# Output powers in four parts behind the weight splits, late softmax scaling in the second attention, and conditioning pieces one block later

## Time and profile before

| | |
|---|---|
| median of 3 runs | 1544.14 us (1543.37 to 1545.25) |
| profiled execution, its own time | 1544.38 us |
| its span, first to last instruction | 1542.5 us |
| mean granted TensorE clock | 0.977 of full |
| PE busy (matmul) | 1457.6 us, 94% |
| DVE, ACT, POOL busy | 749.0, 614.5, 406.1 us |

### The profile page before, as it was taken

How to read it: one execution, slowest core, us unless ns; L and a number is a source line. 1 busy time by engine, 2 the same in 40 slices (tenths; PEclk the granted TensorE clock), 3 DMA queues, 4 the chain that set the end, 5 groups by cost and what they waited for, 6 DMA issues and landing times.

```text
span 1542.5 us, 25177 instructions
## 1 busy us (share of the span) xinstructions
PE 1457.6 (94%) x10880; PEld 1253.0 (81%) x10880; DVE 749.0 (49%) x921; ACT 614.5 (40%) x753; POOL 406.1 (26%) x324
## 2 busy tenths in 40 slices
PE   5799999988999997999799999999999989899999
PEld 5688889988999995765276888888886855799999
DVE  7975645365545466567654121212124577443343
ACT  4433364434333456121345222322224447544443
POOL 4977712100002410000000232343230020134553
PEclk9899999999999998999899999999999989999999
DMA  7466676544655564886434323222233310345552
GB/s 256 164 219 211 221 240 219 203 160 137 191 179 178 189 219 159 265 239 189 151 109 166 108 84 106 87 105 98 93 109 110 101 64 1 110 137 191 172 184 82
DMA packets 158259, 239.37 MB, mean 155 GB/s; under 512 B 5680, under 2 KB 128592, under 8 KB 158032
## 3 DMA queue, kind: packets, MB, share of 16 engines
q1 hardware_dynamic: 153360, 232.85, 45.4%
q10 hardware_dynamic: 4800, 5.08, 1.4%
HBM read 227.55 MB, written 1.05 MB: 148 GB/s over the span
## 4 chain that ended last, share of the span: by engine, by line
PE 84%; DVE 7%; ACT 6%; issue 2%; DMA 1%; POOL 0%; DVEq 0%; SPq 0%; ACTq 0%; POOLq 0%
PE bank L1968 24%; PE bank L1969 24%; PE bank L1970 24%; PE bank L2036 2%; PE bank L2273 2%; ACT A L589 1%; DVE wlo L1085 1%; ACT whi L633 1%; ACT ahi L593 1%; PE bank L2433 1%; PE bank L2110 1%; DVE stat L1713 1%; PE bank L563 1%; PE bank L544 1%; PE bank L2145 1%
## 5 line engine op out<-in xcount | busy, mean ns | idle before, releaser
L1968 PE MATMUL bank<-ahi,whi 128*128 128x256 f32 (+1 forms) x2480 | 792.7, 320 | 38.5 <-DVE wlo L1085 10.3
L1969 PE MATMUL bank<-alo,whi 128*128 128x256 f32 (+1 forms) x2480 | 784.1, 316 | 0.0
L1970 PE MATMUL bank<-ahi,wlo 128*128 128x256 f32 (+1 forms) x2480 | 783.4, 316 | 0.0
L1085 DVE TENSOR_TENSOR wlo<-raw,whi 128x2048 fp32r<-128x2048 f32 x158 | 362.2, 2292 | 533.1 <-ACT whi L633 533.0
L633 ACT ACTIVATE whi<-raw 128x2048 fp32r<-128x2048 f32 x160 | 306.3, 1914 | 726.2 <-PE bank L1970 726.2
L1968 PEld LDWEIGHTS bank<-ahi,whi 128*128 128x128 f32 x2480 | 477.8, 193 | 85.9 <-issue 40.9
L1970 PEld LDWEIGHTS bank<-ahi,wlo 128*128 128x128 f32 x2480 | 477.9, 193 | 28.8
L1969 PEld LDWEIGHTS bank<-alo,whi 128*128 128x128 f32 x2480 | 478.2, 193 | 27.8 <-issue 0.2
L1906 POOL TENSOR_TENSOR alo<-A,ahi 128x512 fp32r<-128x512 f32 (+1 forms) x43 | 125.8, 2927 | 351.8 <-ACT ahi L833 351.8
L1924 POOL TENSOR_TENSOR A<-A 128x512 f32 (+1 forms) x48 | 96.6, 2025 | 442.7 <-ACT A L956 442.7
L1560 DVE SCALAR_TENSOR_TENSOR A<-A,decay 128x512 f32<-128x512 f32 x80 | 53.8, 749 | 0.0
(11 more groups left out here) (302 smaller groups left out, 1200.8 us busy)
## 6 DMA issues: line engine op xcount, KB each, us to landing
raw<-in_w_ff SPq DMA_DIRECT2D x64, 1024.0 KB, 5.2
A<-in_w_mod SPq DMA_DIRECT2D x60, 512.0 KB, 4.7
raw<-in_w_in SPq DMA_DIRECT2D x28, 1024.0 KB, 8.2
modraw<-in_w_mod SPq DMA_DIRECT2D x36, 512.0 KB, 4.8
raw<-in_pw SPq DMA_DIRECT2D x12, 1024.0 KB, 8.4
raw<-in_w_ffn_gate SPq DMA_DIRECT2D x11, 1024.0 KB, 5.3
raw<-in_w_ffn_up SPq DMA_DIRECT2D x11, 1024.0 KB, 5.3
raw<-in_w_ffn_down SPq DMA_DIRECT2D x11, 1024.0 KB, 4.9
```

Source lines behind the costliest of these rows:

```text
L1085: dve.tensor_tensor(wlo[:, k % 2, :], raw[:, (k + 2) % 4, :], whi[:, k % 2, :].bitcast(F32), ALU.subtract).then_inc(wlo_ready, 1)
L1968: pe.matmul(out_, w_hi, a_hi, start=start, stop=False, **kw)
L1969: pe.matmul(out_, w_hi, a_lo, start=False, stop=False, **kw)
L1970: return pe.matmul(out_, w_lo, a_hi, start=False, stop=stop, **kw)
```

## The change

1. **Output powers.** DVE no longer makes those of batch 0 ahead of its block loop. Steps (3, 4) and (5, 6, 7) of batches 0 and 1 stand in the loop at l = 2, 3, 4, 5, each behind that l's `ahead`, so behind the splits of blocks 4 to 7.
2. **Convolution stage.** On PE, block 0 keeps pieces 4 to 7 only, and block l >= 1 has pieces 6 + 2l and 7 + 2l. Pieces 22, 23, 24 and 25 stand between `convolve(5)` and `convolve(6)`, 26 and 27 between the last two channel sums, 28 and 29 behind the sums of squares. Channel sums 4 and 5 come before `convolve(6)`, sum 6 before pieces 26 and 27. On ACT `ahead` stands before `mod_rows`. SP's program is unchanged.
3. **Second attention.** The probabilities are transposed and weighed unscaled. PE spreads the reciprocals over 64 rows with two small matmuls a step, ACT copies them to SBUF (`gspread`), DVE multiplies the 128x256 output of a pair of steps (`gnorm`), then ACT rounds (`gout`) and DVE subtracts (`glo`), one iteration later than before. From step 4 on, DVE copies one of the two transposed banks.
4. **Splits.** wlo of blocks 0 and 1 of "wo" is made by DVE (iteration 17, and behind the loop), not by POOL; ACT makes whi of block 1 in iteration 10.

```
             def act_pw1(p):
                 h = p.least // 2
+                ahead(p)
                 if p.least in (0, 4):
                     mod_rows(1, p.least // 4)
-                ahead(p)
...
                         act.wait_ge(pt_done, TR + i - 1)
+                        act.wait_ge(pn_ready, TR + i - 1)
...
                 if i >= 2:
                     act.wait_ge(o_done, TR + i - 1)
-                for s in range(2):
-                    c = act.activation(ptg[:, i % 2, 512 * s:512 * s + 512], pb[4 + s][:, :], ACT.Copy)
-                c.then_inc(pt_ready, 1)
+                if i < 4:
+                    act.activation(ptg[:, i % 2, 512:1024], pb[5][:, :], ACT.Copy).then_inc(pt_ready, 1)
+                act.activation(ptg[:, i % 2, 0:512], pb[4][:, :], ACT.Copy).then_inc(pt_ready, 1)
+
+            def gspread(c):
+                act.wait_ge(o_done, TR + 2 * c + 2)
+                if c >= 1:
+                    act.wait_ge(olo_ready, TR + 2 * c - 1)
+                act.activation(spd, pb[6 + c % 2][:, 256:512], ACT.Copy).then_inc(ohi_ready, 1)
 
             def gout(c):
-                act.wait_ge(o_done, TR + 2 * c + 2)
-                act.activation(ahi[:, 256 * c:256 * c + 256], pb[6 + c % 2][:, 0:256], ACT.Copy).then_inc(ohi_ready, 1)
-
-            for i in range(1, GSTEPS + 4):
+                act.wait_ge(olo_ready, TR + 2 * c + 1)
+                act.activation(ahi[:, 256 * c:256 * c + 256], onorm, ACT.Copy).then_inc(ohi_ready, 1)
+
+            for i in range(1, GSTEPS + 5):
                 if i - 1 < GSTEPS:
                     gexp(i - 1)
                 if i >= 5 and i % 2:
-                    gout((i - 5) // 2)
+                    gspread((i - 5) // 2)
+                if i >= 6 and i % 2 == 0:
+                    gout((i - 6) // 2)
                 if 0 <= i - 2 < GSTEPS:
                     gpt(i - 2)
-            ahead(Pos(FIRST["qkv"] + 5, 5))
+                if i == 10:
+                    ahead(Pos(FIRST["qkv"] + 5, 5))
...
-            dve.wait_ge(z_ready, 1)
-            dve.wait_ge(ssm_landed, 32)
-            output_powers(0, 3, 8)
...
                 ahead(Pos(l, l))
-                if l in (3, 4):
-                    output_powers(1, *((3, 5), (5, 8))[l - 3])
+                if l == 2:
+                    dve.wait_ge(z_ready, 1)
+                    dve.wait_ge(ssm_landed, 32)
+                if 2 <= l < 6:
+                    output_powers((l - 2) // 2, *((3, 5), (5, 8))[l % 2])
...
-            def gscale(i):
+            def ginvert(i):
                 s0, s1 = 20 + 2 * (i % 2), 36 + 2 * (i % 2)
                 dve.wait_ge(exp_done, TR + 2 * (i + 1))
-                link(dve.reciprocal(stat[:, s1:s1 + 2], stat[:, s0:s0 + 2]))
-                for b in range(2):
-                    m = dve.tensor_scalar(pg[:, i % 2, b, :], pg[:, i % 2, b, :], stat[:, s1 + b:s1 + b + 1],
-                                          None, ALU.mult)
-                m.then_inc(pn_ready, 1)
+                if i >= 2:
+                    dve.wait_ge(o_done, TR + i - 1)
+                dve.reciprocal(stat[:, s1:s1 + 2], stat[:, s0:s0 + 2]).then_inc(pn_ready, 1)
+
+            def gptb(i):
+                dve.wait_ge(pt_done, TR + i + 1)
+                dve.wait_ge(o_done, TR + i - 1)
+                dve.tensor_copy(ptg[:, i % 2, 512:1024], pb[5][:, :]).then_inc(pt_ready, 1)
+
+            def gnorm(c):
+                dve.wait_ge(ohi_ready, TR + 2 * c + 1)
+                if c >= 1:
+                    dve.wait_ge(olo_ready, TR + 2 * c)
+                dve.tensor_tensor(onorm, pb[6 + c % 2][:, 0:256], spd, ALU.mult).then_inc(olo_ready, 1)
...
                 if 0 <= i - 2 < GSTEPS:
-                    gscale(i - 2)
+                    ginvert(i - 2)
+                    if i - 2 >= 4:
+                        gptb(i - 2)
+                if i >= 6 and i % 2 == 0:
+                    glo((i - 6) // 2)
                 if i >= 5 and i % 2:
-                    glo((i - 5) // 2)
+                    gnorm((i - 5) // 2)
+                if i == GSTEPS + 1:
+                    ahead(Pos(FIRST["qkv"] + 4, 4))
+            ahead(Pos(FIRST["qkv"] + 5, 5))
...
-            split_ahead(4)
-            split_ahead(5)
...
                 if l == 0:
                     mod_pieces(4, 4)
-                mod_pieces(8 + 2 * l, 2)
+                else:
+                    mod_pieces(6 + 2 * l, 2)
             convolve(4)
             pe.wait_ge(u_ready, KD)
             for c in range(2):
                 channel_sum(c)
             convolve(5)
-            for c in range(2, 4):
+            for c in range(2, 5):
                 channel_sum(c)
+            mod_pieces(22, 2)
+            channel_sum(5)
+            mod_pieces(24, 2)
             convolve(6)
             mod_turn(1, 2)
-            mod_pieces(24, 2)
             convolve(7)
-            channel_sum(4)
-            channel_sum(5)
+            channel_sum(6)
             mod_pieces(26, 2)
-            channel_sum(6)
             channel_sum(7).then_inc(msum_done, 1)
-            mod_pieces(28, 2)
...
+            mod_pieces(28, 2)
             pe.wait_ge(lrstd_ready, 1)
...
             def gturn(i):
-                pe.wait_ge(pn_ready, TR + i + 1)
+                pe.wait_ge(exp_done, TR + 2 * (i + 1))
                 if i >= 1:
-                    pe.wait_ge(pt_ready, TR + i)
+                    pe.wait_ge(pt_ready, TR + 2 * i)
...
-                pe.wait_ge(pt_ready, TR + i + 1)
+                s1 = 36 + 2 * (i % 2)
+                pe.wait_ge(pn_ready, TR + i + 1)
...
+                for b in range(2):
+                    pe.matmul(pb[6 + c % 2][64 * b:64 * b + 64, 256 + P * qt:256 + P * qt + P],
+                              stat[:, s1 + b:s1 + b + 1].broadcast_to([P, 64]), C["ident"], start=True, stop=True)
+                pe.wait_ge(pt_ready, TR + 2 * (i + 1))
...
-            pe.wait_ge(olo_ready, TR + 8)
+            pe.wait_ge(olo_ready, TR + 16)
```

More of the change, by code:

```diff
@@ L211, in program @@
         ptg = area(11776, 2048).rearrange("p (r w) -> p r w", r=2)
+        spd = area(13824, 256)
+        onorm = area(14080, 256)
         pb = [ctx.enter_context(nc.psum_tensor(f"bank{n}", [P, 512], F32)) for n in range(8)]
@@ L1715, in gmax @@
                 dve.tensor_scalar(stat[:, s0:s0 + 2], stat[:, s1:s1 + 2], -0.125, None, ALU.mult).then_inc(nmax_ready, 1)
-            def gscale(i):
+            def ginvert(i):
                 s0, s1 = 20 + 2 * (i % 2), 36 + 2 * (i % 2)
                 dve.wait_ge(exp_done, TR + 2 * (i + 1))
-                link(dve.reciprocal(stat[:, s1:s1 + 2], stat[:, s0:s0 + 2]))
-                for b in range(2):
-                    m = dve.tensor_scalar(pg[:, i % 2, b, :], pg[:, i % 2, b, :], stat[:, s1 + b:s1 + b + 1],
-                                          None, ALU.mult)
-                m.then_inc(pn_ready, 1)
+                if i >= 2:
[10 more added lines that the diff above has]
+                dve.tensor_tensor(onorm, pb[6 + c % 2][:, 0:256], spd, ALU.mult).then_inc(olo_ready, 1)
             def glo(c):
-                dve.wait_ge(ohi_ready, TR + c + 1)
-                dve.tensor_tensor(alo[:, 256 * c:256 * c + 256], pb[6 + c % 2][:, 0:256],
+                dve.wait_ge(ohi_ready, TR + 2 * c + 2)
+                dve.tensor_tensor(alo[:, 256 * c:256 * c + 256], onorm,
                                   ahi[:, 256 * c:256 * c + 256].bitcast(F32), ALU.subtract).then_inc(olo_ready, 1)
-            for i in range(1, GSTEPS + 4):
+            for i in range(1, GSTEPS + 5):
                 if i - 1 < GSTEPS:
@@ L1744, in _ @@
                 if 0 <= i - 2 < GSTEPS:
-                    gscale(i - 2)
+                    ginvert(i - 2)
[3 more added lines that the diff above has]
+                    glo((i - 6) // 2)
                 if i >= 5 and i % 2:
-                    glo((i - 5) // 2)
+                    gnorm((i - 5) // 2)
+                if i == GSTEPS + 1:
+                    ahead(Pos(FIRST["qkv"] + 4, 4))
+            ahead(Pos(FIRST["qkv"] + 5, 5))
             ph[0] = "wo"
-            dve.wait_ge(wlo_ready, FIRST["wo"] + 2)
             for l in range(4):
@@ L1942, in cosine_part @@
                     .then_inc(gq_cos, 1)
[L1944 to L1951, removed]
             pool.wait_ge(gtab_landed, 16)
@@ L2438, in gweigh @@
                 c, qt = i // 2, i % 2
-                pe.wait_ge(pt_ready, TR + i + 1)
+                s1 = 36 + 2 * (i % 2)
+                pe.wait_ge(pn_ready, TR + i + 1)
                 if i >= 4 and qt == 0:
-                    pe.wait_ge(olo_ready, TR + c - 1)
+                    pe.wait_ge(olo_ready, TR + 2 * c - 3)
+                for b in range(2):
+                    pe.matmul(pb[6 + c % 2][64 * b:64 * b + 64, 256 + P * qt:256 + P * qt + P],
+                              stat[:, s1 + b:s1 + b + 1].broadcast_to([P, 64]), C["ident"], start=True, stop=True)
```

(1 more changed line is left out.)

## The result

The changed kernel takes 1554.03 us (median of 4 runs, 1551.93 to 1557.43); the kernel before took 1544.05 beside it. The ratio is 1.006, 95% interval 1.0048 to 1.0071. The forecast was 1539.5, and faster; it came out 10 us slower than the kernel before, 14.5 above the forecast and outside the range of 1532 to 1546. The profiled run took 1551.93 us with a span of 1550.1, against 1544.38 and 1542.5. It is the fastest of the four, so the trace explains +7.6 us; the other 2.4 us between it and the +10.0 of the medians lie in the spread of the runs, and no trace shows them.

A forecast was written before the change was run, and what follows sets the result against it. PE, busy 94% of the span, was taken as the bound, with time to win only in its waits or low clock. The terms' -4.4 us from 1544.38 gave 1540.0, 1539.7 as median; stated 1539.5, range 1532 to 1546.

The forecast's parts named there:

- so that starts at 723.1 - 8.6 = 714.5: Convolution stage: everything on PE up to `convolve(4)` comes 8.6 us earlier, so `convolve(4)` starts at 714.5.
- 3.5 to landing: Convolution stage: SP's last-pair copies land, and `convolve(6)` starts, 3.5 us behind the last issue.
- my 739.1 for `convolve(6)`: Convolution stage: loads out at 729.6, 6 us of copies and 3.5 to landing start `convolve(6)` at 739.1.
- The issue of eight copies: Convolution stage: SP issues the last pair's eight copies in 6 us, between 4.7 and 7.3.
- the restart behind this wait: Convolution stage: low PE clock after about 8 us idle ahead of `convolve(6)`, charged +1.7 us.
- the late copies: Rival, convolution stage: SP's eight copies need 16 us, `convolve(6)` starts at 749, part 2 costs +8.5, total 1549.5; 9%.
- slow restart again at the new place, +2.0 us: First phase: PE restarts at a low clock after idling at `ssm_y(0)` for POOL, charged +2.0 us.
- the bound of 4.3 us at half clock: First phase: the old restart behind block 4's split, at least 4.3 us at half clock, 2.1 us of work lost.
- its upper bound of 4.1: Output powers: the most part 1 could cost, with one more split (+2.1) and the full +2.4 restart.
- Step 5's scores: Second attention: PE starts step 5's scores at 1267.8 against 1275.67, 7.9 us ahead.
- The chain of `gnorm`, `gout`, `glo`: Second attention's end: with this chain behind the last exponentials, "wo" starts at 1316.1 against 1320.58, -4.5 us.
- +1.6 - 1.5 - 4.5 = -4.4: Whole kernel: output powers +1.6, convolution stage -1.5, second attention with the splits -4.5, together 4.4 us faster.

The follow-up runs named there:

- kernel 4: The changed kernel, with SP issuing its shift copies of pairs 2 and 3 ahead of the mod loads of iterations 5 and 7: 1533.78 us.
- kernel 2: The kernel before with only the convolution stage's new order (PE's mod pieces and channel sums, ACT's `ahead` before `mod_rows`): 1550.94 us.
- 11: The changed kernel, with only SP's last pair of shift copies (l == 7) moved ahead of its mod loads: 1540.22 us.
- kernel 1: The kernel before with only DVE's lines on the output powers changed: 1550.66 us.
- kernel 6: The kernel before with the output powers changed and the first `ssm_y` on PE one block later (l == 9): 1541.10 us.
- kernel 3: The kernel before with only the second attention and the "wo" splits changed: 1542.69 us.
- 10: The kernel before with the second attention and splits changed, and "wo"'s first block waiting for its input chunk by chunk: 1539.34 us.
- kernel 7: The kernel before with only SP's shift copies of pairs 2 and 3 moved ahead of the mod loads: 1545.85 us.
- 5: The kernel before with the convolution stage's new order and SP's shift copies of pairs 2 and 3 ahead of the mod loads: 1531.55 us.
- 12: The kernel before with only the first `ssm_y` on PE one block later: 1544.60 us.
- 8: The changed kernel, with SP's copies of pairs 2 and 3 ahead of the mod loads and the first `ssm_y` one block later: 1525.30 us.
- kernel 9: The changed kernel, with SP's copies of pairs 2 and 3 earlier, first `ssm_y` one block later and "wo" waiting chunk by chunk: 1522.51 us.

## Why the prediction was wrong

**The step that failed** is in part 2: "so that starts at 723.1 - 8.6 = 714.5", and with it the "3.5 to landing". The first took PE's side alone. SP's queue was read for the last pair, not for pair 2, whose copies `convolve(4)` needs and which stand behind the loads of pieces 22 and 23 in just the same way; those wait for pieces 18 and 19, which PE now uses behind block 6 and its two convolutions. The second was taken from one case and held fixed: 3.5 us behind the last issue. With it pair 2 would have landed at 713.75 + 3.5 = 717.3, ahead of PE at 718.6, and even a sum that had read the queue would have seen no wait there; it took 8.4. The wait of 3.5 us came, and 2.8 us of slow clock in the 40 matmuls behind it. All that follows on PE is then late, and so are the last pair's copies. From there the chain is as predicted: my 739.1 for `convolve(6)` is 743.2 with the 4.15 us by which the stage was entered late; it started at 751.83. The 8.6 us between are 3.5 + 2.8, 2.1 more from the last issue to the start (5.6, the step had 3.5), and 0.2. The issue of eight copies was put at 6 us and took 6.18, and the restart behind this wait at 1.7 and took 1.6. Both hits are luck in part: kernel 4 gives 5.47 and 9.54 us for such issues, and the restart does not follow the length of the wait (last section). Part 2: -1.5 predicted, +6.4 from the two instructions (10.58 - 4.15), +6.2 by kernel 2. Kernels 4 and 11 show that both waits go with the place of the copies in SP's queue. What makes a copy land in 8.7 us there and in 4.6 before was not tried by itself.

The rival "the late copies" had the right sign and place, but the wrong cause: it wanted copies of 2 us each. Each issue was quick; they began late, and the copies landed later behind their issue.

**Part 1** had the right mechanism, and a term that was too small, the "slow restart again at the new place, +2.0 us". No wait for split 4, a wait of 7.28 us at `ssm_y(0)`, `h_ready` at 105.6 (predicted 105.8), PE on at 105.78 (106.0), one split more ahead of it. The restart was put at +2.0 from the bound of 4.3 us at half clock; the rows above show 0.50 until 112 and 0.66 until 114, and the instruction behind the phase is +2.9, where +1.6 was predicted: with the 0.66 us that PE was early at `ssm_y`, the restart cost 3.6. Then 1.2 us more went between 208.93 and 600.85: 1.5 of them near 330, where the clock is low (last section), which was not in the sum at all, less 0.3 elsewhere. By kernel 1 the whole part costs 6.0, above its upper bound of 4.1; its trace has +6.2 at the entry of the convolution stage where the changed kernel's has +4.2, with the same first phase. That this was the price of the wait and of the clock behind it, not of the powers, kernel 6 shows: +6.0 with `ssm_y(0)` behind block 8, -4.2 with it behind block 9.

**Parts 3 and 4** had the right mechanism, and a term was left out. Step 5's scores come 8.3 us earlier relative to the stage's entry (7.9), the steps are 3.61 (3.61), "wo" starts 3.8 us earlier (4.5). The chain of `gnorm`, `gout`, `glo` was in the sum, as the start of "wo"; missing was that PE waits 2.75 us for it and restarts slowly, which costs 1.2 us (kernels 3 and 10). By kernel 3 the parts give 2.0 us, not 4.5.

**The sum.** Predicted +1.6 - 1.5 - 4.5 = -4.4. From the followed instructions: +2.9 + 1.2 + 6.4 - 0.4 - 3.8 + 1.2 = +7.5, and +7.6 unrounded, the difference of the two spans; the -0.4 lies between 817.87 and 1260.15. Of the 12.0 us of error part 2 is 7.9, and the clock (part 1's restart, 330, "wo") nearly all the rest; terms of about 1 us are no larger than what two traces differ by.

The range was too narrow for a sum with three waits that move: each had been costed by its own walk through the queues, and a mistake in a walk is not inside its bounds.

## What to carry to other kernels

When work that frees buffers is moved later on one engine, list every instruction that stands in the loading engine's queue behind the waits for those buffers, for each iteration and not for the last one alone; a transfer that does not need the buffer should stand ahead of the one that does, and its time to landing is to be read where it will stand, not where it stood. A wait that is removed shows the next engine's lateness: here a block of independent work ahead of the new wait turned +6.0 us into -4.2. And wait for a chain's results piece by piece where the consumer takes them piece by piece, above all where the clock falls in the wait.

## What the runs showed of the hardware

The price of the clock behind a wait differed more than I had thought: behind 7.28 us of wait it stayed at 0.50 for some 6 us and cost 3.6 us (changed kernel), behind 10.27 us of wait it cost 1.6 us in `convolve(6)`, behind 3.50 us of wait 2.8 us in `convolve(4)`. The longer wait was not the dearer one. Equal waits at the same place differ too: behind 3.49 us ahead of `convolve(6)` the kernel before keeps the full clock (4.50 us), behind 3.83 us there kernel 7 loses 1.7 us (6.20 us, clock 0.50 in 740 to 742).

Between 320 and 356 us, in a stage that no part of the change touches, with the same two PE waits of 2.05 and 2.28 us in most of the kernels, the clock was 1.00 in all seven profiles of kernels without part 1 (before, 2, 3, 5, 7, 10, 12) and 0.86 to 0.95 in all seven with it (changed, 1, 4, 6, 8, 9, 11). The first of the two waits ends between 326.50 and 328.80 us in the former, between 331.12 and 332.25 or between 321.67 and 322.60 in the latter. So the low clock at these waits goes with part 1, and with the time at which they come, by a few microseconds. No run separates the two, and why is open. The windows of kernel 9 and of kernel 7 in that stretch:

```profile
320.00:356.00 36.00, 28.70 (x267) 27.87 (x268) 21.51 (x27) 16.75 (x18) 0.00 (x0) 0.86 0.45 144
```

```profile
320.00:356.00 36.00, 30.02 (x301) 29.17 (x299) 22.57 (x23) 16.16 (x17) 0.00 (x0) 1.00 0.52 164
```
